# Second norm in one three-operand step per tile, split there, and a written-out first up-projection iteration

## What is computed

```python
h2 = rms_norm(x, lp['norm2_g']) * (1.0 + scale2) + shift2
up, ffn_buf_new = causal_dwconv(h2 @ lp['w_up'], ffn_buf, lp['ffn_conv_w'], lp['ffn_conv_b'])
val, gt = jnp.split(up, 2, axis=-1)
x = x + gate2 * ((jax.nn.gelu(gt) * val) @ lp['w_down'])
```

## Time and profile before

| | |
|---|---|
| median of 3 runs | 986.07 us |
| lowest and highest | 982.07, 986.3 us |
| the profiled execution's own time | 985.16 us |
| its span, first to last instruction | 983.4 us |
| PE, DVE, ACT, POOL busy | 96%, 67%, 54%, 20% of the span |
| mean granted TensorE clock | 0.983 of full |

### The profile page before, as it was taken

How to read it: one execution, slowest core, us unless ns; L and a number is a source line. 1 busy time by engine, 2 the same in 40 slices (tenths; PEclk the granted TensorE clock), 3 DMA queues, 4 the chain that set the end, 5 groups by cost and what they waited for, 6 DMA issues and landing times.

```text
span 983.4 us, 20621 instructions
## 1 busy us (share of the span) xinstructions
PE 945.4 (96%) x7984; PEld 881.0 (90%) x7984; DVE 656.3 (67%) x1253; ACT 526.5 (54%) x1183; POOL 192.8 (20%) x192
## 2 busy tenths in 40 slices
PE   4799999899999999999999999999999999999997
PEld 2488876699999999999898989999999999999997
DVE  2695278478988988989873576777777777722221
ACT  2332854399889898898873333444444443312110
POOL 0022222133334333433340230010001001000000
PEclk9799999899999999999999989999999999999999
DMA  9968642400202202122121432333333332652202
GB/s 326 340 200 253 199 155 82 156 1 23 87 23 108 87 23 88 54 77 87 44 65 45 108 58 66 104 87 85 85 85 85 95 106 59 165 146 60 63 3 87
DMA packets 106289, 100.13 MB, mean 102 GB/s; under 512 B 7119, under 2 KB 94943, under 8 KB 104126
## 3 DMA queue, kind: packets, MB, share of 16 engines
q1 hardware_dynamic: 102422, 77.91, 27.2%
q0 software_dynamic: 3456, 20.97, 6.0%
q10 hardware_dynamic: 340, 0.27, 0.1%
HBM read 96.41 MB, written 2.94 MB: 101 GB/s over the span
## 4 chain that ended last, share of the span: by engine, by line
PE 88%; DVE 5%; ACT 3%; DMA 2%; issue 1%; SPq 0%; POOL 0%; DVEq 0%; ACTq 0%
PE ps L909 51%; PE ps L1297 19%; PE ps L904 7%; PE ps L942 2%; PE ps L1204 2%; PE ps L1255 2%; DMA RW<-w_ada 2%; PE ps L1292 1%; PE ps L1079 1%; PE ps L1230 1%; PE ps L915 1%; DVE normed_low L1904 1%; DVE RB L1878 0%; ACT RB L1493 0%; DVE RB L2334 0%
## 5 line engine op out<-in xcount | busy, mean ns | idle before, releaser
L909 PE MATMUL ps<-normed_high,up_weights_high 128*128 128x260 f32 x704 | 142.3, 283 | 0.2
L909 PE MATMUL ps<-normed_high,up_weights_low 128*128 128x260 f32 x704 | 142.0, 283 | 0.0
L909 PE MATMUL ps<-normed_low,up_weights_high 128*128 128x260 f32 x704 | 141.8, 283 | 0.0
L849 POOL TENSOR_TENSOR latents_low<-RB,latents_high 128x512 fp32r<-128x512 f32 (+1 forms) x72 | 86.2, 1197 | 163.9 <-ACT latents_high L1628 159.7
L1744 ACT ACTIVATE up_weights_high<-RW 128x1024 fp32r<-128x1024 f32 x44 | 46.5, 1060 | 133.5 <-PE ps L909 133.5
L1297 PE MATMUL ps<-key_weights_high,latents_high 128*128 128x260 f32 x528 | 116.4, 302 | 0.8 <-ACT RB L1675 0.7
L909 PEld LDWEIGHTS ps<-normed_high,up_weights_high 128*128 128x128 f32 x704 | 108.6, 189 | 0.8 <-DVE normed_low L1904 0.6
L909 PEld LDWEIGHTS ps<-normed_high,up_weights_low 128*128 128x128 f32 x704 | 108.6, 189 | 0.0
L909 PEld LDWEIGHTS ps<-normed_low,up_weights_high 128*128 128x128 f32 x704 | 108.3, 188 | 0.0
L1297 PE MATMUL ps<-key_weights_low,latents_high 128*128 128x260 f32 x528 | 106.4, 283 | 0.0
L1297 PE MATMUL ps<-key_weights_high,latents_low 128*128 128x260 f32 x528 | 106.4, 283 | 0.0
(11 more groups left out here) (331 smaller groups left out, 2197.1 us busy)
## 6 DMA issues: line engine op xcount, KB each, us to landing
RW<-w_ada SPq DMA_DIRECT2D x24, 1024.0 KB, 7.2
RW<-w_up SPq DMA_DIRECT2D x44, 512.0 KB, 5.0
RW<-w_down SPq DMA_DIRECT2D x8, 1408.0 KB, 7.2
RW<-w_in SPq DMA_DIRECT2D x11, 512.0 KB, 8.2
RB<-w_o SPq DMA_DIRECT2D x8, 512.0 KB, 4.1
RB<-x_prompt SPq DMA_DIRECT2D x2, 1024.0 KB, 13.3
o_y_p<-RB SPq DMA_DIRECT2D x4, 512.0 KB
cst<-consts SPq DMA_DIRECT2D x1, 845.0 KB, 11.6
```

The source lines that it names most:

```text
L849: nc.gpsimd.tensor_tensor(latL[:, g % 3, c:4 * P], turned[:, g % 3, c:4 * P], latH[:, g % 3, c:4 * P].bitcast(F32), ALU.subtract).then_inc ...
L909: last = mm(ps[j % 4][rows[0]:rows[1], h, 0:H], lhsT, src[:, h * H:(h + 1) * H], start=start, stop=stop)
```

## The change

The second norm now makes of each tile's prompt columns, on DVE, `x * gain * rs` in one three-operand instruction (`scaled`); POOL has no part in it. ACT adds the shift alone and writes the rounded high part `hH` directly. DVE takes the low part in a second three-operand instruction, `(scaled + shift) - hH` (`normed_low`). DVE runs `scaled` two tiles ahead of `normed_low`. The samples' columns are normed, rounded and split once for all tiles, ahead of the first `normed_low`, with a semaphore of their own (`s_dec2`).

On PE the first lap of the up-projection is written out. The first two jobs, value and gate of the first hidden tile, are claimed together; value runs tile by tile as normed tiles come, and from tile 4 on each value tile is followed by a gate tile (0 to 3), with gate tiles 4 to 7 at the end. Jobs 2 and 3 follow, and the loop runs laps 1 to 10. The 8 scratch matmuls ahead of the up-projection are gone.

```diff
--- before.py
+++ after.py
@@ -562,6 +562,7 @@
         s_wihi = sem("input_weights_high")
         s_wilo = sem("input_weights_low")
         s_hlo = sem("normed_low")
+        s_dec2 = sem("samples_second_normed")
         s_hha = sem("normed_high_by_scalar")
         s_n1 = sem("first_squares_added")
         s_dec = sem("samples_normed")
@@ -884,10 +885,6 @@
                         cached_latents((u + 1) % 2, u + 1)
                         new_latent((u + 1) % 2, u + 1)
             add_squares(0, KT - 1, KT + 12, 0)
-
-            pool.wait_ge(s_rs, 7)
-            for k in range(KT // 2, KT):
-                nc.gpsimd.tensor_tensor(h2[:, k, 0:NP], xT[:, k, 0:NP], rs[:, 0:NP], ALU.mult).then_inc(s_hq, 1)
 
             with pool.Fori(0, FT // 2) as i:
                 for e in range(2):
@@ -1400,20 +1397,38 @@
             for m in range(2 * FT):
                 last = tr(flat(j)[:, 2 * NS * m:2 * NS * m + 2 * NS], fs_tok[:, P * m:P * m + P], 2 * NS)
             last.then_inc(psum_full[j % 4], 1)
-            claim(pe, up_job(0), 0)
-            keep_busy(flat(up_job(0))[:, 0:2 * P], 8)
-
-            with pe.Fori(0, FT // 2) as i:
+
+            def up_products(e, g, k):
+
+                last = three(up_job(2 * e + g), wuH, wuL, KT * g + k, hH, hL, k, k == 0, k == KT - 1)
+                if k == KT - 1:
+                    last.then_inc(psum_full[up_job(2 * e + g) % 4], 1)
+
+            def up_start(e, g, i):
+
+                claim(pe, up_job(2 * e + g), i)
+                pe.wait_ge(s_wlo, 4 * i + 2 * e + g + 1)
+
+            up_start(0, 0, 0)
+            up_start(0, 1, 0)
+            pe.wait_ge(s_dec2, 1)
+            for k in range(KT):
+                pe.wait_ge(s_hlo, KT + k + 1)
+                up_products(0, 0, k)
+                if k >= KT // 2:
+                    up_products(0, 1, k - KT // 2)
+            for k in range(KT // 2, KT):
+                up_products(0, 1, k)
+            for g in range(2):
+                up_start(1, g, 0)
+                for k in range(KT):
+                    up_products(1, g, k)
+            with pe.Fori(1, FT // 2) as i:
                 for e in range(2):
                     for g in range(2):
-                        j = up_job(2 * e + g)
-                        claim(pe, j, i)
-                        pe.wait_ge(s_wlo, 4 * i + 2 * e + g + 1)
+                        up_start(e, g, i)
                         for k in range(KT):
-                            if e == 0 and g == 0:
-                                pe.wait_ge(s_hlo, KT + k + 1)
-                            last = three(j, wuH, wuL, KT * g + k, hH, hL, k, k == 0, k == KT - 1)
-                        last.then_inc(psum_full[j % 4], 1)
+                            up_products(e, g, k)
 
             for m in range(KT):
                 j = J_DOWN[m]
@@ -1755,11 +1770,8 @@
             act.wait_ge(s_mix, 2 * LT)
             rstd(J_N2, D).then_inc(s_rs, 1)
             for k in range(KT):
-                if k < KT // 2:
-                    act.wait_ge(s_hp, KT + k + 1)
-                else:
-                    act.wait_ge(s_hq, k + 1 - KT // 2)
-                A(h2[:, k, 0:NP], h2[:, k, 0:NP], ACT.Identity, bias=modT[:, 3 * KT + k, 0:1], scale=gmod[:, k, 0:1]).then_inc(s_h, 1)
+                act.wait_ge(s_hp, KT + k + 1)
+                A(hH[:, k, 0:NP], h2[:, k, 0:NP], ACT.Identity, bias=modT[:, 3 * KT + k, 0:1]).then_inc(s_h, 1)
 
             act.wait_ge(s_pads, 2)
 
@@ -2329,18 +2341,27 @@
             st.seq(V.tensor_tensor(gmod[:, :, :], gmod[:, :, :], pr("norm2_g", 0, KT).unsqueeze(2).to_broadcast([P, KT, 9]), MUL))
             dve.wait_ge(s_rs, 7)
 
+            def scaled(k):
+
+                V.scalar_tensor_tensor(h2[:, k, 0:NP], xT[:, k, 0:NP], gmod[:, k, 0:1], rs[:, 0:NP], MUL, MUL).then_inc(s_hp, 1)
+
+            def normed_low(k):
+
+                dve.wait_ge(s_h, KT + k + 1)
+                V.scalar_tensor_tensor(hL[:, k, 0:NP], h2[:, k, 0:NP], modT[:, 3 * KT + k, 0:1], hH[:, k, 0:NP].bitcast(F32), ADD, SUB).then_inc(s_hlo, 1)
+
             dec = h2[:, :, NP:T]
-            for k in range(KT // 2):
-                V.tensor_tensor(h2[:, k, 0:NP], xT[:, k, 0:NP], rs[:, 0:NP], MUL).then_inc(s_hp, 1)
-                if k > 0:
-                    st.need(st.n)
-                if k == 0:
-                    st.did(V.tensor_tensor(dec, xT[:, :, NP:T], rs[:, NP:T].unsqueeze(1).to_broadcast([P, KT, NS]), MUL))
-                elif k == 1:
-                    st.did(V.tensor_tensor(dec, dec, gmod[:, :, 1:9], MUL))
-                elif k == 2:
-                    st.seq(V.tensor_tensor(dec, dec, modT[:, 3 * KT:4 * KT, 1:9], ADD))
-            split_normed(h2, hL, KT)
+            scaled(0)
+            st.seq(V.tensor_tensor(dec, xT[:, :, NP:T], rs[:, NP:T].unsqueeze(1).to_broadcast([P, KT, NS]), MUL))
+            st.seq(V.tensor_tensor(dec, dec, gmod[:, :, 1:9], MUL))
+            st.seq(V.tensor_tensor(dec, dec, modT[:, 3 * KT:4 * KT, 1:9], ADD))
+            scaled(1)
+            st.seq(V.tensor_copy(hH[:, :, NP:T], dec))
+            V.tensor_tensor(hL[:, :, NP:T], dec, hH[:, :, NP:T].bitcast(F32), SUB).then_inc(s_dec2, 1)
+            for k in range(KT):
+                normed_low(k)
+                if k + 2 < KT:
+                    scaled(k + 2)
 
             full(dve, J_FST)
             V.tensor_copy(FS[:, :, :].rearrange("p m n -> p (m n)"), flat(J_FST)[:, 0:4 * FT * NS]).then_inc(psum_free[J_FST % 4], 1)
```

## The result

The changed kernel takes 989.26 us in the median of 20 runs (986.83 to 991.57), against 985.57 for the kernel before in 20 runs beside it (982.07 to 987.38): a ratio of 1.0041, interval 1.0032 to 1.0050. That is 3.7 us more, inside the band that was called no change and in the middle of the range; the forecast was 989.6. The interval leaves 1 out, so the loss is real, if small.

A forecast was written before the change was run, and what follows sets the result against it. The prediction took PE's unbroken run of matmuls to bound the kernel, so a later start moves the end: 985.16 + 2.2 (wait for ps1) + 2.2 (low clock) = 989.6 us, range 985.5 to 993.0.

The forecast's parts named there:

- The norm's steps: On DVE, three-operand steps 0.67 apart, 1.34 us a tile; the eighth low part ends at 586.85, 3.7 us sooner than before.
- The wait that takes it back: PE's first product waits for DVE's copy out of ps1, starting at about 587.7 instead of 584.67: +2.2 us.
- The clock: Without scratch matmuls the first products meet PE's half clock: +2.2 us, from returns of 3.1 and 5.7 us; ends 0 and 3.4.
- What covers it: Third job's weights, 2.5 us of rounding and splitting, are covered with about 1.1 us left; otherwise part of a microsecond lost.
- The sum: Whole kernel: 985.16 of the profiled execution + 2.2 + 2.2 = 989.6 us, a small loss inside the no-change band.
- The full clock: Rival: PE's clock is not low at the first products or returns at once; only the buffer's wait counts, 987.4; chance 0.10.
- the long low clock: Rival: PE's clock stays low 5.5 us or more in the first two jobs; 991.1 or 992.0, clearly slower; chance 0.25.
- the buffer does not hold PE: Rival: PE starts behind the transposes at about 578.6 and takes tiles as they come; 979.3 us; chance 0.03.

The follow-up runs named there:

- e3: The changed kernel with PE as before (8 scratch matmuls, loop of 11 laps, one claim a job), so the new norm alone: 983.45 us, 0.9980 of the kernel before.
- e1: The changed kernel with DVE's copy of the convolution state out of ps1 behind the second low part, not the eighth: 982.71 us, 0.9975 of the kernel before.
- e6: The changed kernel with the gate job claimed right ahead of its first tile, not ahead of value's first: 985.22 us, 0.9997 of the kernel before.
- e7: The changed kernel with the up-projection's four buffers rotated by two, value and gate first in ps2 and ps3: 980.48 us, 0.9954 of the kernel before.
- e2: The changed kernel with 12 scratch matmuls put back on PE ahead of the first two claims: 987.87 us, 1.0021 of the kernel before.
- e4: The kernel before, old norm kept, with PE as changed (both claims first, interleaved tiles, no scratch matmuls): 992.67 us, 1.0078 of the kernel before.
- e8: The changed kernel with buffers rotated by two and all gate tiles behind all value tiles: 981.81 us, 0.9965 of the kernel before.
- e5: The changed kernel with the convolution state in ps3 instead of ps1 and the output projection's last jobs renumbered: 983.15 us, 0.9981 of the kernel before.

## Why the prediction was right

**The norm's steps.** Right. The three-operand steps took 0.74 to 0.75 (the first head group's 0.752 was the row), the low parts stood 1.33 apart against 1.34, and the eighth ended 12.05 us after DVE's first step against 12.29 forecast. e3 shows it alone, as a small gain.

**The wait that takes it back.** Right, and shown by three kernels: e1 moves the copy and the start follows it, e6 has the copy named, e7 changes buffers alone and the wait is gone. The first product came 13.06 after DVE's first step, forecast 13.14; the term was 2.2 and is 2.1.

**The clock.** Right in kind, 0.8 too large in size. The term stood at 2.2, the mean of two stretches; it is 1.40 by the profile of the changed kernel, 1.4 by the medians of e2. Its reason holds: the scratch work had sat through the low level, and now the products do; e2 puts scratch work back and takes the price away. Two things made the term smaller. The low stretch of products was 3.5 us, near the 3.1 at 45 us and far from the 5.7. And a pair of matmuls takes 0.43 at half clock against 0.24, so 0.44 of the low time is lost, not half: 3.5 x 0.44 = 1.5. That it came out so near the 3.1 is chance: behind a wait of 3.36 us, as long as the one at 45 us, e6's products took about 5 us at the low level, and e1's, behind 2.63 us, 4.5. The rows before the change did not fix the size better than the mean that was taken.

The Trainium skill (TensorE: Matmul & The Clock Gate, section "HAM oscillation — how this bites in real kernels") says that matmuls behind an idle gap pay for the clock's return. The trace of e6 agrees: there the level fell in the 3.36 us gap of the late claim, and the products behind it paid. In the changed kernel the products behind 9.19 us of idling pay too, but the level was at 0.50 before the idling began. The forecast counted 578 us as agreeing as well; there PE had waited only 0.51 us, so that place does not show the rule.

**What covers it.** The weights of the third job cost nothing: the chain shows 2112 matmuls from the first product on without a wait.

**The sum.** 2.2 + 2.2 = 4.4 was forecast and 3.48 measured in the profile, 3.7 between medians. That 989.6 lies so near 989.26 is partly luck: the sum was made from an execution 0.4 under the later median of the kernel before, and an excess of 0.7 over the difference of the medians more than made that up.

**The rivals.** The full clock is excluded by the windows, the long low clock by its 3.5 us. That the buffer does not hold PE did not happen; e7 is what it would have been: the forecast put that case 5.9 us below the kernel before, e7 lies 5.0 below.

## What to carry to other kernels

Before several outputs are begun together, look up the last reader of each one's buffer: claims moved ahead of a matmul make it wait for the slowest of them, and a copy that cost nothing at its place becomes the start of everything. Turning the buffers by two was worth 8.8 us here, and rewriting the norm 2.1. Where a profile names a releaser that had long been done, look what else the instruction waits for, and make a kernel in which that wait stands alone.

## What was not expected of the hardware

The clock fell while PE was hardly idle. In the kernel before:

```profile
577.00:577.50 0.50, 0.50 (x11) 0.50 (x9) 0.50 (x2) 0.19 (x1) 0.50 (x2) 0.86 1.21 288
577.50:578.00 0.50, 0.50 (x8) 0.50 (x7) 0.50 (x2) 0.00 (x0) 0.50 (x1) 0.50 0.47 107
```

PE worked on its 44 transposes from 575.23 to 578.58, and had waited 0.51 us ahead of them. So the low level of the earlier trace rows began at about 577.4, a microsecond before the scratch work. It is the same in the changed kernel (between 578.0 and 578.5) and in e2, e3, e4, e7 and e8: the level falls while the transposes run. In e7 it is 1.00 to 577 and 0.50 from 578, with the transposes from 575.71 to 579.24 and no wait of PE above 0.90 us between 545 and there. In e1 and e6 it fell 0.3 and 0.8 us behind the transposes. In e5 it stayed at 1.00 with products that started 3.36 us after DVE's first step:

```profile
577.50:580.50 3.00, 2.85 (x44) 2.79 (x44) 2.86 (x9) 1.44 (x2) 0.00 (x0) 1.00 1.19 282
580.50:586.00 5.50, 4.15 (x26) 3.31 (x26) 5.50 (x9) 2.89 (x4) 0.00 (x0) 1.00 0.00 0
```

Why it held there, with PE waiting for tiles for a quarter of the second stretch, and not in the other nine, stays open. So does the time to the return: counted from the first product behind PE's wait it was 3.5 us in the changed kernel, 4.5 in e1 and about 5 in e6; in e7, where PE did not wait, more than 6 from the fall on.
